# A hybrid decoder layer on one NeuronCore: layer norms that scale four blocks at a time and store their own result

## What is computed

```python
x = layer_norm(DEEP_ALPHA * x + 0.5 * swiglu_1(x), ln1_g, ln1_b)
x = layer_norm(DEEP_ALPHA * x + concat([att, gdn]) @ w_o, ln2_g, ln2_b)
x = layer_norm(DEEP_ALPHA * x + 0.5 * swiglu_2(x), ln3_g, ln3_b)

def layer_norm(x, g, b):
    mu = mean(x, -1); var = mean(square(x - mu), -1)
    return (x - mu) * rsqrt(var + LN_EPS) * g + b
```

## Time and profile before

| | us |
|---|---|
| median of 3 runs (lowest to highest) | 3196.95 (3196.69 to 3202.11) |
| the profiled execution's own time | 3196.57 |
| its span, first to last instruction | 3194.9 |
| PE busy | 2867.2 (90%) |
| DVE busy | 1491.4 (47%) |
| ACT busy | 880.6 (28%) |
| POOL busy | 199.2 (6%) |

### The profile page before, as it was taken

How to read it: one execution, slowest core, us unless ns; L and a number is a source line. 1 busy time by engine, 2 the same in 40 slices (tenths; PEclk the granted TensorE clock), 3 DMA queues, 4 the chain that set the end, 5 groups by cost and what they waited for, 6 DMA issues and landing times. The chain is left out here.

```text
span 3194.9 us, 44597 instructions
## 1 busy us (share of the span) xinstructions
PE 2867.2 (90%) x17430; PEld 2600.0 (81%) x17444; DVE 1491.4 (47%) x2356; ACT 880.6 (28%) x1406; POOL 199.2 (6%) x374
## 2 busy tenths in 40 slices
PE   7999999999869999777888487879699999999996
PEld 6999999999768799653787354559499999999994
DVE  3232232233555678648887576541522233333235
ACT  2111111111213557602454344431331111111112
POOL 0000000000000000122000000750000000000000
PEclk8999999999989999859999699999899999999998
DMA  3111111110031122333000200862021111111101
GB/s 118 40 47 46 46 39 46 46 39 26 19 96 41 43 74 76 115 78 97 27 28 8 94 1 17 242 193 84 19 63 46 47 40 47 40 41 46 42 14 56
DMA packets 265720, 185.68 MB, mean 58 GB/s; under 512 B 62735, under 2 KB 245215, under 8 KB 265542
## 3 DMA queue, kind: packets, MB, share of 16 engines
q1 hardware_dynamic: 214182, 113.52, 12.5%
q0 software_dynamic: 20672, 58.46, 5.4%
q10 hardware_dynamic: 30688, 11.27, 1.3%
HBM read 156.97 MB, written 26.22 MB: 57 GB/s over the span
## 5 line engine op out<-in xcount | busy, mean ns | idle before, releaser
L356 DVE TENSOR_TENSOR ffn_hidden<-ffn_hidden,ffn_ps_b 128x1092 f32<-128x1092 f32 x44 | 56.9, 1292 | 400.4 <-PE ffn_ps_b L84 400.4
L310 ACT ACTIVATE ffn_h_hi<-ffn_hidden 128x1092 fp32r<-128x1092 f32 x44 | 49.2, 1119 | 496.6 <-DVE ffn_hidden L356 496.6
L295 ACT ACTIVATE ffn_hi_d<-ffn_raw_d 128x1024 fp32r<-128x1024 f32 x40 | 42.5, 1063 | 495.8 <-PE ffn_ps_b L84 379.9
L84 PE MATMUL ffn_ps_a<-mixer_mix_hi,ffn_hi_g 128*128 128x364 f32 x528 | 118.1, 332 | 24.4 <-DVE ffn_lo_g L339 21.1
L303 ACT ACTIVATE ffn_hidden<-ffn_ps_a 128x1092 f32<-128x1092 f32 x44 | 47.6, 1083 | 289.7 <-PE ffn_ps_a L84 289.7
L84 PE MATMUL ffn_ps_a<-first_x_hi,ffn_hi_g 128*128 128x364 f32 x528 | 117.9, 332 | 5.6 <-DVE ffn_lo_g L339 5.6
L196 POOL DMA_DIRECT2D ffn_raw_d<-in_ffn_w_down x40 | 21.2, 530 | 1586.2 <-DVE ffn_lo_d L345 1401.0
L84 PE MATMUL ffn_ps_a<-first_x_lo,ffn_hi_g 128*128 128x364 f32 x528 | 117.5, 331 | 0.0
L84 PE MATMUL ffn_ps_a<-first_x_hi,ffn_lo_g 128*128 128x364 f32 x528 | 117.5, 331 | 0.0
L84 PE MATMUL ffn_ps_a<-mixer_mix_lo,ffn_hi_g 128*128 128x364 f32 x528 | 117.3, 330 | 0.0
L84 PE MATMUL ffn_ps_a<-mixer_mix_hi,ffn_lo_g 128*128 128x364 f32 x528 | 117.1, 330 | 0.0
(11 more groups left out here) (598 smaller groups left out, 6948.0 us busy)
## 6 DMA issues: line engine op xcount, KB each, us to landing
ffn_raw_d<-in_ffn_w_down POOLq DMA_DIRECT2D x40, 512.0 KB, 3.6
proj_raw<-in_w_in SPq DMA_DIRECT2D x22, 512.0 KB, 3.7
second_ffn_raw_g<-in_ffn_w_gate SPq DMA_DIRECT2D x22, 512.0 KB, 3.9
second_ffn_raw_u<-in_ffn_w_up SPq DMA_DIRECT2D x22, 512.0 KB, 3.6
first_ffn_raw_g<-in_ffn_w_gate SPq DMA_DIRECT2D x21, 512.0 KB
first_ffn_raw_u<-in_ffn_w_up SPq DMA_DIRECT2D x21, 512.0 KB, 3.6
scratch_qkv<-proj_stage POOLq DMA_DIRECT2D x12, 544.0 KB, 3.0
delta_cur<-scratch_qkv SPq DMA_DIRECT2D x8, 768.0 KB, 5.6
```

The lines of the kernel that those rows point to most:

```text
L84: last = pe.matmul(out[:, s, 0:SL], w(k), x(k)[:, s * SL:(s + 1) * SL], start=start and n == 0 and p == 0, stop=stop and n == len(ks) - 1 ...
L295: act.activation(d_hi[:, k, :], raw["d"][:, :], ACT.Copy).then_inc(whi_done["d"], 1)
L310: act.activation(h_hi[:, par, fb, :], act_buf[:, fb, :], ACT.Copy).then_inc(hhi_done, 1)
L356: dve.tensor_tensor(hid, hid, ps_b[:, :, 0:SL], ALU.mult).then_inc(mul_done, 1)
```

## The change

- `three_pass`: the last slice's matmul has 360 columns (`USED`); in each stage that uses it DVE sets the four columns left over in both PSUM tiles to zero, and PE waits for that (`pads_set`).
- `norm`: the root table is loaded by a dummy root at the start. DVE multiplies by `rstd` alone, four blocks in one instruction, twice a slice. ACT then scales by g and adds the bias in place, per block, with two pointers; in ln1 and ln2 one further instruction per four blocks rounds to the high part, and DVE makes the low part of four blocks in one. The order of the slices on ACT and DVE changes, and the variances share two PSUM banks instead of three.
- `res` now holds the normalised value with its bias. So `mixer_output` and the second `ffn` scale it by alpha only; their loads of the bias go. ln1 writes `res` in six DMAs, one per half slice.
- ln3 also stores: PE transposes half tiles (three PSUM banks), DVE copies them (three row buffers), SP writes. `store_tokens` goes.

```diff
+USED = (SL, SL, NT - 2 * SL)
-                last = pe.matmul(out[:, s, 0:SL], w(k), x(k)[:, s * SL:(s + 1) * SL],
+                last = pe.matmul(out[:, s, 0:USED[s]], w(k), x(k)[:, s * SL:s * SL + USED[s]],
...
-def ffn(nc, name, w_gate, w_up, w_down, res, x_hi, x_lo, raws, resid_b=None):
+def ffn(nc, name, w_gate, w_up, w_down, res, x_hi, x_lo, raws, weigh=False):
-            if resid_b is not None:
-                column_load(sp, shift[:, :], resid_b[0], shift_in)
+            pe.wait_ge(pads_set, 2)
             gates(0, 0, first=True)
-                    act.activation(res[:, k, :], res[:, k, :], ACT.Identity, scale=ALPHA, bias=shift[:, k:k + 1]
-                                   ).then_inc(res_scaled, 1)
+                    act.activation(res[:, k, :], res[:, k, :], ACT.Copy, scale=ALPHA).then_inc(res_scaled, 1)
+            for ps in (ps_a, ps_b):
+                dve.memset(ps[:, SLICES - 1, USED[-1]:SL], 0.0).then_inc(pads_set, 1)
             weight_lo("g", 0)
...
-        var = sc.ps("var", [P, SLICES, 512])
+        var = sc.ps("var", [P, 2, 512])
+        if store is not None:
+            turned = sc.ps("turned", [P, 3, 4, P])
+            rows = sc.sb("rows", [P, 3, D])
+        last_slice = [((t + 1) * P - 1 if t < TILES - 1 else NT - 1) // SL for t in range(TILES)]
...
+                    for h in range(2):
+                        sp.wait_ge(s["made"], KT * i + 4 * h + 4)
+                        sp.dma_start(resid_out[4 * h:4 * h + 4, :, cols[i]].rearrange("k p c -> p k c"),
+                                     res[:, 4 * h:4 * h + 4, cols[i]]).then_inc(s["res_out"], 16)
...
+                for t in range(TILES):
+                    sp.wait_ge(s["copied"], 2 * t + 2)
+                    sp.dma_start(dst, rows[0:w, t % 3, :]).then_inc(s[f"out_done{t % 3}"], 16)
...
+            def variances(i):
                 pe.wait_ge(s["squared"], i + 1)
+                if i >= 2:
+                    pe.wait_ge(s["std_done"], i - 1)
...
+            def turn(i):
+                for t in range(TILES):
+                    if last_slice[t] != i:
+                        continue
+                    pe.wait_ge(s["made"], KT * (i + 1))
+                    for half in range(2):
+                        n = 2 * t + half
+                        if n >= 3:
+                            pe.wait_ge(s["copied"], n - 2)
+                        for k in range(4):
+                            last = pe.transpose(turned[0:w, n % 3, k, :], res[:, half * 4 + k, t * P:t * P + w],
+                                                ident[:, :])
+                        last.then_inc(s["turned_done"], 1)
+            means(0)
+            means(1)
+            variances(0)
+            means(2)
+            variances(1)
+            variances(2)
+            if store is not None:
+                for i in range(SLICES):
+                    turn(i)
...
+            def shift(i, h):
+                act.wait_ge(s["squared"], i + 1)
+                act.wait_ge(s["scaled"], 2 * i + h + 1)
+                for k in range(4 * h, 4 * h + 4):
+                    act.activation(res[:, k, cols[i]], res[:, k, cols[i]], ACT.Identity, scale=gb[:, 0, k:k + 1],
+                                   bias=gb[:, 1, k:k + 1]).then_inc(s["made"], 1)
+                if x_hi is not None:
+                    act.wait_ge(s["made"], KT * i + 4 * h + 4)
+                    act.activation(x_hi[:, 4 * h:4 * h + 4, cols[i]], res[:, 4 * h:4 * h + 4, cols[i]], ACT.Copy
+                                   ).then_inc(s["hi_done"], 1)
+
+            act.wait_ge(s["eps_set"], 1)
+            act.activation(table[:, :], eps[:, :], ACT.Sqrt)
             square(0)
             square(1)
             root(0)
             act.wait_ge(s["gb_in"], 32)
+            shift(0, 0)
+            shift(0, 1)
+            square(2)
+            root(1)
+            shift(1, 0)
+            root(2)
+            shift(1, 1)
+            shift(2, 0)
+            shift(2, 1)
...
+            def scale(i):
+                for h in range(2):
+                    r = res[:, 4 * h:4 * h + 4, cols[i]]
+                    dve.tensor_tensor(r, r, rstd[:, i, :].unsqueeze(1).to_broadcast([P, 4, SL]), ALU.mult
+                                      ).then_inc(s["scaled"], 1)
+            def low(i, h):
+                if x_hi is not None:
+                    x = slice(4 * h, 4 * h + 4)
+                    dve.tensor_tensor(x_lo[:, x, cols[i]], res[:, x, cols[i]], x_hi[:, x, cols[i]].bitcast(F32),
+                                      ALU.subtract)
+            def copy(i):
...
+                        dve.wait_ge(s["turned_done"], n + 1)
+                        if t >= 3:
+                            dve.wait_ge(s[f"out_done{t % 3}"], 16 * (t // 3))
+                        dve.tensor_copy(rows[0:w, t % 3, half * 512:half * 512 + 512].rearrange(
+                            "p (k f) -> p k f", k=4), turned[0:w, n % 3, :, :]).then_inc(s["copied"], 1)
             centre(0)
             centre(1)
+            invert(0)
+            scale(0)
+            centre(2)
+            low(0, 0)
+            low(0, 1)
+            invert(1)
+            scale(1)
+            copy(0)
+            low(1, 0)
+            invert(2)
+            scale(2)
+            low(1, 1)
+            copy(1)
+            low(2, 0)
+            low(2, 1)
+            copy(2)
```

More of the change, by code:

```diff
@@ L316, in _ @@
             down_hi(0, first=True)
[L317 to L320, removed]
+            if weigh:
                 for k in range(KT):
-                    act.activation(res[:, k, :], res[:, k, :], ACT.Identity, scale=ALPHA, bias=shift[:, k:k + 1]
-                                   ).then_inc(res_scaled, 1)
+                    act.activation(res[:, k, :], res[:, k, :], ACT.Copy, scale=ALPHA).then_inc(res_scaled, 1)
             def down(d, last, one_left=False):
@@ L443, in square @@
                 act.activation(sq[:, i % 2, :, :], res[:, :, cols[i]], ACT.Square).then_inc(s["squared"], 1)
[L445 to L451, removed]
             def root(i):
                 act.wait_ge(s["var_done"], i + 1)
-                act.activation(rstd[:, cols[i]], var[:, i, 0:SL], ACT.Sqrt, bias=eps[:, :]).then_inc(s["std_done"], 1)
+                act.activation(rstd[:, i, :], var[:, i % 2, 0:SL], ACT.Sqrt, bias=eps[:, :]
+                               ).then_inc(s["std_done"], 1)
+            def shift(i, h):
[10 more added lines that the diff above has]
+            act.activation(table[:, :], eps[:, :], ACT.Sqrt)
             square(0)
             square(1)
-            act.wait_ge(s["eps_set"], 1)
             root(0)
             act.wait_ge(s["gb_in"], 32)
[L462 to L465, removed]
-                root(i)
-                high(i)
+            shift(0, 0)
[7 more added lines that the diff above has]
+            shift(2, 1)
         @block.vector
@@ new lines, in low @@
+            def low(i, h):
+                if x_hi is not None:
+                    dve.wait_ge(s["hi_done"], 2 * i + h + 1)
+                    dve.wait_ge(s["made"], KT * i + 4 * h + 4)
+                    x = slice(4 * h, 4 * h + 4)
+                    dve.tensor_tensor(x_lo[:, x, cols[i]], res[:, x, cols[i]], x_hi[:, x, cols[i]].bitcast(F32),
+                                      ALU.subtract)
+            def copy(i):
+                for t in range(TILES):
+                    if store is None or last_slice[t] != i:
+                        continue
+                    w = tile_width(t)
+                    for half in range(2):
+                        n = 2 * t + half
+                        dve.wait_ge(s["turned_done"], n + 1)
[3 more added lines that the diff above has]
+                            "p (k f) -> p k f", k=4), turned[0:w, n % 3, :, :]).then_inc(s["copied"], 1)
@@ L2923, in scale_residual @@
             def scale_residual():
-                act.wait_ge(s["shift_in"], 16)
-                act.activation(shift[:, :], shift[:, :], ACT.Copy, scale=ALPHA).then_inc(s["shift_made"], 1)
-                act.wait_ge(s["shift_made"], 1)
                 act.wait_ge(s["res_in"], 16 * KT)
                 for k in range(KT):
-                    act.activation(res[:, k, :], res[:, k, :], ACT.Identity, scale=ALPHA, bias=shift[:, k:k + 1]
+                    act.activation(res[:, k, :], res[:, k, :], ACT.Copy, scale=ALPHA
                                    ).then_inc(s["res_scaled"], 1)
```

112 lines of the change are left out of this document (31 added, 81 removed).

## The result

The changed kernel takes 3169.94 us in the median of four runs (3163.90 to 3171.59) against 3196.82 us before: ratio 0.991, 95% interval [0.9898, 0.9922]. That is 26.9 us less, where 21.3 were forecast. A second set of five runs, taken later as a control, gave 3173.00 against 3197.89 us, 0.9922 [0.9908, 0.9936], 24.9 us less. The profiled execution took 3170.46 us, its span 3168.8 us.

The account below looks back on a forecast made before the run. Matmuls bound the feed-forward; in norms and store the chain of engines handing work on counts. Terms 6.7 + 11.8 + 1.4 + 0.8 + 0.6 = 21.3 us less gave 3175.6 us, range 3168 to 3184 us.

Parts of the forecast that it names:

- Narrower slice: Three-pass matmuls: 4032 of 12096 stream 360 instead of 364 columns, 1.67 ns each, 6.7 us less.
- fixed extra: Three-pass matmuls: the unexplained 15 ns above 364 columns' time doesn't grow with columns, so four columns are worth 1.67 ns.
- The first rival: Three-pass matmuls: columns don't set the 167 ns, so 6.7 us are missing, 3182.3 us; chance 0.17.
- rate for pairs: Three-pass matmuls: the skill's sustained rate for load and matmul pairs, 0.13 ns per column, giving 2.1 us in all.
- The third rival: Three-pass matmuls: changing width costs 0.08 us a group, 323 us lost, about 3505 us; chance 0.04.
- the step on the dropped shift: Output projection: shorter residual scaling ends TensorE's wait 0.6 us earlier; the dropped shift loads are worth nothing.
- the fourth rival: Better case: ACT's small instructions take 0.50 us, transposes avoid half clock, columns count 1.83 ns; about 3170.8 us, chance 0.10.
- Last norm and store: Last norm and store: early root table, wide scales and fused store save 12.8 us, net 11.8 after slow transposes.
- the forecast's replay: Last norm: the new order replayed on the trace's own times, last store issued at 3178.4 instead of 3191.16 us.
- the price that the forecast named: Last norm, DVE: half-tile copies ahead of the third reciprocal make it start 2 us later than root 2 would allow.
- First and second norm: First two norms: ACT gains work, DVE loses some; 1.4 us gained in the second, 0.8 us in the first.
- Residual scaling: Output projection: eight scalings without bias pointer, each 0.07 to 0.1 us shorter, end TensorE's wait 0.6 us earlier.

Follow-up runs that it names:

- e2_norms_only: The changed kernel with 364 columns in every slice and no zeroed columns: 3181.16 us, ratio 0.995 to the kernel before.
- the first set: Runs taking the change apart: narrower slice alone on the kernel before, 3189.68 us; everything but the slice, 3181.16 us; slices of 368, 368 and 352, 3175.83 us.
- e5_gap_back: The changed kernel with an unused 32-byte gap where the dropped shift tile stood, in both feed-forwards and output projection: 3175.79 us, ratio 0.9944.
- e8_late_table: The changed kernel without the small root at each norm's start, so the root table loads where root 0 needs it: 3165.15 us, one run.
- e11_square_first_again: The changed kernel with square 2 and root 1 between slice 0's shift halves in the first two norms, low parts later, repeated: 3162.55 us, 0.989.

## Why the prediction was right

The side, the likeliest case and the range held; 26.9 us came where 21.3 were forecast, 24.9 in the control. The terms for the narrower slice, the norms and the store had the right mechanism and nearly the right size; one term of 0.6 us did not show, and one effect of some 5 us had no term.

**Narrower slice**: the term of 6.7 us, with its fixed extra, held: 7.3 us alone, 40 ns a block. The first rival (columns don't count) would have left 3196.8 us and fell. The Trainium skill (TensorE: Matmul & The Clock Gate, section "Back-to-back issue gap") has the spacing of a lone matmul grow by the column over 2.4 GHz, which would also give 6.7 us, and agrees with this slope; the 2.1 us estimated from its rate for pairs lie outside the 4.5 to 10.5 us of the interval. The third rival, a price on changing width, fell with the same run.

**What failed is the step on the dropped shift**: it counted the instructions and loads that go away and called the loads worth nothing, and it did not ask where the next buffers come to lie. The tile's 32 bytes moved the weights, and 6912 matmuls (44 gate and up blocks in each feed-forward and 8 blocks of the output projection, 72 in each) became 0.7 ns closer: about 5 us, which no term had. The effect belongs to the move and the narrower slice together. The mean spacing of the gate and up matmuls is 166.8 ns before, 166.7 with the move alone (e2_norms_only, whose matmuls are otherwise those of before), 166.3 narrowed alone and 165.6 with both; so at the new place narrowing is worth 1.1 ns a matmul and not 0.5, and the two halves of the first set had to fall short of the whole. With the place given back, the kernel takes 3175.79 us; the forecast was 3175.6. That it comes so close is in part luck, since a median carries some two us. The time of the fourth rival (3170.8) thus came true, but not by its reasons: the shifts take the 0.58 us of the forecast, not 0.50; whether the four columns are worth 1.67 or 1.83 ns these runs can't tell.

**Last norm and store**: 14.9 us in the profile, against 11.8 net, and nearly all of the difference is the clock. The profiled execution of before began its means and variance 2 at half clock: granted clock 0.69 in the first 3.3 us of the means and 0.50 in the first 2.9 us of variance 2, which took 6.66 us. That of the changed kernel ran both at 1.00, the means in 10.02 and variance 2 in 5.16 us. The means before:

```profile
3123.63 11.72 PE L423 MATMUL ln_mean<-second_res,main_ones_mean 128*128 128x364 f32 x32 [2.67 <-PEq L3132]
3130.50 3.19 DVE L473 TENSOR_TENSOR second_res<-second_res,ln_mean 128x2912 f32<-128x2912 f32 x1 [6.38 <-PE ln_mean L423]
```

The first centring starts 6.87 us behind the first matmul there and 5.17 us here: 1.7 us. The run e5_gap_back has the changed kernel's last norm and met half clock at both places (granted clock 0.56 and 0.66 in the first 3.7 and 3.0 us):

```profile
3119.29 11.72 PE L439 MATMUL ln_mean<-second_res,main_ones_mean 128*128 128x364 f32 x32 [2.52 <-PEq L3163]
3126.15 3.19 DVE L521 TENSOR_TENSOR second_res<-second_res,ln_mean 128x2912 f32<-128x2912 f32 x1 [6.77 <-PE ln_mean L439]
3149.45 6.85 PE L448 MATMUL ln_var<-ln_sq,main_ones_mean 128*128 128x364 f32 x16 [2.45 <-ACT ln_sq L483]
3159.18 2.42 DVE L527 RECIPROCAL ln_rstd<-ln_rstd 128x364 f32<-128x364 f32 x1
3174.97 0.54 SPq L431 DMA_DIRECT2D out_y_sample<-ln_rows  x1
```

With its first matmul set at the time of that before, every step of the forecast's replay is met within 0.3 us, from reciprocal 0 (3142.2 us for 3142.3) to the end of scale 2 (3169.2 for 3169.1). Reciprocal 2 starts 2.2 us behind root 2's end, the price that the forecast named, the last store is issued 55.7 us behind the first matmul, which is 54.7 and the 1.0 for slow transposes, and the stage takes 59.6 us: 11.7 us less than before. In the control the stage takes 59.4 us. So the forecast's term is right for the clock that it assumed, and some three of the profile's 14.9 us are the clock of that execution. The clock follows the run and not the change: behind the same pause of 2.52 us this norm's means ran at full clock in some runs of the same code and at half clock in others (DVE waits 5.08 us for the first mean in the changed kernel and 6.77 us in e5_gap_back). In the first norm, too, it waits 5.08 us here and 6.77 us in the runs of e8_late_table and e11_square_first_again.

**First and second norm**: 1.4 us for the second, exact. In the first, DVE ends 55.15 us behind the first matmul, and the next stage's loads begin 2.9 us after its last low part starts, the residual's store landing last as foreseen. These loads begin 56.4 us behind the first matmul, and 58.9 us before; 1.7 of the 2.5 us are again the clock of the first means, which leaves the 0.8 us of the forecast.

**Residual scaling**: eight instructions take 8.16 instead of 8.89 us, 0.09 each, as taken. But TensorE's wait behind them was 2.07 us, not shorter than 1.58; in the control it was 1.60. Over all runs it was 1.26 to 3.93 us with the shorter scaling and 1.58 to 3.37 with the longer one. So the 0.6 us did not show: the scaling starts when the residual has landed, and that came 15.7 us behind the stage's first matmul before, 17.9 in the changed kernel and 17.2 in the control.

## What to carry to other kernels

Taking a tile away moves every tile allocated behind it, and in stages of thousands of packed matmuls a fraction of a nanosecond each is as large as the change one meant to make: look at the spacing position by position, and put a gap in the tile's place before crediting the gain. Where a chain runs through several engines, replay it on the trace's own durations; it gave three stages here to a few tenths at the clock that it assumed, and named the order that beat the change. Fusing a store into the stage ahead of it was worth some 11 us here; the waits for row buffers were half of it. And before a profile's surplus is credited to a change, compare the granted clock at the same steps in several runs.

## What the runs showed that was not expected

- The spacing of packed matmuls at full clock depends, by up to 25 ns at single positions and 0.7 ns in the mean, on where weights and activations lie against each other in the on-chip memory; a move of both together (the down projection, whose weights and hidden activations moved by the same 32 bytes) changed single positions by some 1 ns at most, and a move of 256 bytes gave the same pattern back. With 364 columns in all slices the same move of 32 bytes showed in single positions, by up to 9 ns, and hardly in the mean (166.8 and 166.7 ns).
- The same code, entered after the same pause of TensorE, starts at half or at full clock from run to run, 1.7 us a norm; variance 2 of the last norm does the same behind a pause of 2.45 us (5.16 and 6.85 us).
- The table load of 1.28 us costs 0.96 us on the chain where a wait of 0.36 us covers a part of it; behind that wait, as before, it cost 1.4 us.
